# Forget gates of a streaming encoder step: float32 matmuls in four column blocks with a summing product, in place of 128-column float32r matmuls

## The reference, cut to what matters

```python
xn = rmsnorm(h, g_pre_mix)                    # h: (tokens, 1024)
y = jnp.einsum('bld,de->ble', xn, w_in)       # ... q_a | k_a | v_a | f_a (8 columns) | q_b ...
logf = jax.nn.log_sigmoid((f_a + b_forget).astype(jnp.float32))
# FoX: s = q k * scale + c_q - c_k, with c = cumsum(logf), causal; softmax; times v
```

## Time and profile before

| | |
|---|---|
| Median of 3 runs | 1680.81 us (1680.64 to 1680.95) |
| The profiled execution's own time | 1680.76 us |
| Its span (first to last instruction) | 1679.0 us |
| Granted TensorE clock, mean | 0.999 of full speed |
| TensorE busy | 1651.5 us (98%) |
| VectorE, ScalarE, GpSimd busy | 1083.5 us (65%), 775.8 us (46%), 310.2 us (18%) |
| DMA engines, mean over the span | 122 GB/s |

### The profile page before, as it was taken

How to read it: one execution, slowest core, us unless ns; L and a number is a source line. 1 busy time by engine, 2 the same in 40 slices (tenths; PEclk the granted TensorE clock), 3 DMA queues, 4 the chain that set the end, 5 groups by cost and what they waited for, 6 DMA issues and landing times.

```text
span 1679.0 us, 27411 instructions
## 1 busy us (share of the span) xinstructions
PE 1651.5 (98%) x9540; PEld 1489.3 (89%) x9540; DVE 1083.5 (65%) x2322; ACT 775.8 (46%) x1630; POOL 310.2 (18%) x438
## 2 busy tenths in 40 slices
PE   8999999999999999999999999999999999999998
PEld 8999999999999988989988899888888888888886
DVE  7556666553999744454445597888877667774744
ACT  6477777765777533352233333222222334443521
POOL 1311111115333211124532230000000000000242
PEclk9999999999999999999999999999999999999999
DMA  5221212231222554563443422444432763444641
GB/s 187 77 61 41 79 47 59 67 110 36 74 57 67 163 179 160 160 210 123 147 140 111 134 85 94 131 144 144 144 131 105 258 220 111 132 149 125 192 163 75
DMA packets 164314, 205.34 MB, mean 122 GB/s; under 512 B 16152, under 2 KB 113240, under 8 KB 164208
## 3 DMA queue, kind: packets, MB, share of 16 engines
q1 hardware_dynamic: 164208, 203.97, 38.0%
HBM read 144.85 MB, written 57.28 MB: 120 GB/s over the span
## 4 chain that ended last, share of the span: by engine, by line
PE 80%; DVE 9%; ACT 4%; issue 4%; POOL 2%; DMA 0%; DVEq 0%; ACTq 0%; SPq 0%; POOLq 0%
PE gb L503 8%; PE gb L3173 6%; PE gb L2290 5%; PE sc L3173 5%; PE gb L2825 4%; PE gb L2661 4%; PE sc L2825 4%; PE tp L3173 4%; PE tp L2825 4%; PE tp L798 3%; PE sc L2449 3%; PE tp L2449 3%; PE gb L930 3%; PE gb L931 2%; PE gb L932 2%
## 5 line engine op out<-in xcount | busy, mean ns | idle before, releaser
L930 PE MATMUL gb<-Xh,wh 128*128 128x384 f32 (+1 forms) x504 | 175.9, 349 | 0.0
L489 POOL TENSOR_TENSOR wl<-raw,wh 128x256 fp32r<-128x256 f32 x168 | 125.0, 775 | 264.2 <-ACT wh L474 175.4
L931 PE MATMUL gb<-Xh,wl 128*128 128x384 f32 (+1 forms) x504 | 170.7, 339 | 0.0
L932 PE MATMUL gb<-Xl,wh 128*128 128x384 f32 (+1 forms) x504 | 170.7, 339 | 0.0
L3297 POOL TENSOR_TENSOR wl<-raw,wh 128x1024 fp32r<-128x1024 f32 x2 | 5.3, 2626 | 559.0 <-ACT wh L3288 559.0
L503 PE MATMUL gb<-Xh,wh 128*128 128x384 f32 (+1 forms) x288 | 103.9, 361 | 0.0
L503 PE MATMUL gb<-Xh,wl 128*128 128x384 f32 (+1 forms) x288 | 97.4, 338 | 0.0
L503 PE MATMUL gb<-Xl,wh 128*128 128x384 f32 (+1 forms) x288 | 97.3, 338 | 0.0
L930 PEld LDWEIGHTS gb<-Xh,wh 128*128 128x128 f32 x504 | 95.0, 189 | 0.1
L931 PEld LDWEIGHTS gb<-Xh,wl 128*128 128x128 f32 x504 | 95.0, 188 | 0.0
L932 PEld LDWEIGHTS gb<-Xl,wh 128*128 128x128 f32 x504 | 94.8, 188 | 0.0
(11 more groups left out here) (548 smaller groups left out, 4777.4 us busy)
## 6 DMA issues: line engine op xcount, KB each, us to landing
zr<-u_scr SPq DMA_DIRECT2D x91, 256.0 KB, 3.0
raw<-in_w_in SPq DMA_DIRECT2D x70, 256.0 KB, 3.2
u_scr<-ustore SPq DMA_DIRECT2D x26, 576.0 KB, 3.6
u_scr<-ustore SPq DMA_DIRECT2D x13, 768.0 KB, 3.2
sig_scr<-sig SPq DMA_DIRECT2D x16, 576.0 KB, 3.1
raw<-in_w_up SPq DMA_DIRECT2D x36, 256.0 KB, 4.4
kc<-in_cache_fox_k SPq DMA_DIRECT2D x8, 1024.0 KB, 5.6
vc<-in_cache_fox_v SPq DMA_DIRECT2D x8, 1024.0 KB, 7.6
```

What stands on the lines that cost most here:

```text
L489: nc.gpsimd.tensor_tensor(wl[U.slot][:, q], raw[U.slot][:, q], wh[U.slot][:, q].bitcast(F32), ALU.subtract).then_inc(w_lo if x == 3 else w ...
L930: nc.tensor.matmul(gb[c][:, 0:x1 - x0], wh[U.slot][:, ws], Xh3[:, k, x0:x1], start=(k == 0), stop=False)
L931: nc.tensor.matmul(gb[c][:, 0:x1 - x0], wl[U.slot][:, ws], Xh3[:, k, x0:x1], start=False, stop=False)
L932: last = nc.tensor.matmul(gb[c][:, 0:x1 - x0], wh[U.slot][:, ws], Xl3[:, k, x0:x1], start=False, stop=(k == KT - 1))
```

## The change

The forget gates are multiplied in plain float32. `fw3` becomes 8 blocks of 32 columns (8 of weights, 24 of zeros), kept in `sig`; only 32 columns are loaded (`f_parts`). The 16 matmuls of `gates(c)` write four row groups of the bank: block k goes to rows 32(k mod 4) to 32(k mod 4)+31, so that each group sums two of the eight blocks, and four matmuls in a row go to four different groups. ACT copies all 128 rows of the bank into `f_sums`, which is `nB` (`f_sum_act`), and a 17th float32 matmul with a matrix of four small identities (`f_pick`, 8 columns) adds the four groups: `f_pick_pe(c)`, put behind `first(c)`. It writes rows 0 to 7 of the same bank, and DVE adds the bias from there. The turns move: 7, 8 and 9 are all in `first(1)`.

```diff
--- before.py
+++ after.py
@@ -377,7 +377,8 @@
 
 
 
-        fw = PTl[:, 8 * P:16 * P]
+        f_sums, f_pick, f_tmp = nB, sig[:, 0:8], sig[:, 16:64]
+        fw = sig[:, 64:320]
         fw3 = fw.rearrange("p (k n) -> p k n", k=KT)
         fbank = [po, gb[2], po]
 
@@ -400,8 +401,8 @@
         cst_in, cst_r, id_in, gpre_in = sem("cst_in"), sem("cst_r"), sem("id_in"), sem("gpre_in")
         x_in = [sem(f"x_in{t}") for t in range(10)]
         g_in, ssq_done, rstd_done, x_chain = sem("g_in"), sem("ssq_done"), sem("rstd_done"), sem("x_chain")
-        bf_in, lf_low, f_zero = sem("bf_in"), sem("lf_low"), sem("f_zero")
-        sq_done, xs_done, x_hi, x_lo = sem("sq_done"), sem("xs_done"), sem("x_hi"), sem("x_lo")
+        bf_in, f_summed, f_zero = sem("bf_in"), sem("f_summed"), sem("f_zero")
+        sq_done, xs_done, x_hi, f_picked = sem("sq_done"), sem("xs_done"), sem("x_hi"), sem("f_picked")
         lf_chain, lf_act, lf_done, cum_out = sem("lf_chain"), sem("lf_act"), sem("lf_done"), sem("cum_out")
         ckb_in = [sem(f"ckb_in{h}") for h in range(2)]
         zero_s, one_set, tail_zero = sem("zero_s"), sem("one_set"), sem("tail_zero")
@@ -448,6 +449,11 @@
             cs_ = bass.ds(reg * step + c0, P) if step else slice(c0, c0 + P)
             return [(lambda d: d[:, 0:4, :], v[:, 0:4, cs_]), (lambda d: d[:, 4:8, :], v[:, 4:8, cs_])]
 
+        def f_parts():
+
+            v = I["w_in"].rearrange("(k p) n -> p k n", p=P)[:, :, COL_F:COL_F + 32]
+            return [(lambda d: d[:, 0:4, 0:32], v[:, 0:4, :]), (lambda d: d[:, 4:8, 0:32], v[:, 4:8, :])]
+
         def cols_qb(reg):
 
             v = I["w_in"].rearrange("(k p) n -> p k n", p=P)
@@ -539,7 +545,7 @@
             rows_in(0, 1)
             sp.dma_start(gpre[:, :], I["g_pre_mix"].to_broadcast([P, D])).then_inc(gpre_in, 16)
             rows_in(2, 3)
-            load(sp, Unit(U_F), cols_of(I["w_in"], COL_F))
+            load(sp, Unit(U_F), f_parts())
             rows_in(4)
             load(sp, Unit(1), cols_of(I["w_in"], COL_QA))
             rows_in(5, 6, 7, 8, 9)
@@ -585,7 +591,7 @@
             square(3)
             root(1)
             high(0)
-            f_hi_act(act)
+            f_copy_act(act)
             high(1)
             square(4)
             high(2)
@@ -602,23 +608,35 @@
             square(9)
             high(6)
             root(4)
-            f_low_act(act, 0)
+            f_sum_act(act, 0)
             high(7)
             high(8)
-            f_low_act(act, 1)
+            f_sum_act(act, 1)
             high(9)
 
 
-        def f_hi_act(act):
+        def f_rows(k0):
+            return fw3[:, k0:k0 + 4, 0:8], raw[0][:, :].rearrange("p (k n) -> p k n", k=KT)[:, k0:k0 + 4, 0:8]
+
+        def f_copy_act(act):
             act.wait_ge(raw_full[0], 32)
             act.wait_ge(f_zero, 1)
-            nc.scalar.activation(fw3[:, :, 0:8], raw[0][:, :].rearrange("p (k n) -> p k n", k=KT)[:, :, 0:8],
-                                 ACT.Copy).then_inc(w_hi, 1)
-
-        def f_lo_pool(pool):
+            to, src = f_rows(0)
+            nc.scalar.activation(to, src, ACT.Copy).then_inc(w_hi, 1)
+
+        def f_copy_pool(pool):
+            pool.wait_ge(raw_full[0], 32)
+            pool.wait_ge(f_zero, 1)
             pool.wait_ge(w_hi, 1)
-            nc.gpsimd.tensor_tensor(fw3[:, :, 32:40], raw[0][:, :].rearrange("p (k n) -> p k n", k=KT)[:, :, 0:8],
-                                    fw3[:, :, 0:8].bitcast(F32), ALU.subtract).then_inc(w_lo, 1)
+            to, src = f_rows(4)
+            nc.gpsimd.tensor_copy(to, src).then_inc(w_lo, 1)
+
+        def f_pick_dve(v):
+            four_id = ident[:, :].rearrange("p (g r) -> p g r", g=4)
+            two = f_tmp[:, 0:16].rearrange("p (g r) -> p g r", g=2)
+            nc.vector.tensor_tensor(two, four_id[:, 0:2, 0:8], four_id[:, 2:4, 0:8], ALU.add).then_inc(f_zero, 1)
+            v.wait_ge(f_zero, 2)
+            nc.vector.tensor_tensor(f_pick, f_tmp[:, 0:8], f_tmp[:, 8:16], ALU.add).then_inc(f_zero, 1)
 
         def hi_second(act):
             act.wait_ge(raw_full[0], 64)
@@ -671,9 +689,10 @@
                                             ALU.subtract).then_inc(tp_free[h], 1)
 
             nc.vector.memset(small[:, :], 1.0).then_inc(x_chain, 1)
-            nc.vector.memset(fw.bitcast(F32), 0.0).then_inc(f_zero, 1)
+            nc.vector.memset(fw, 0.0).then_inc(f_zero, 1)
             v.wait_ge(id_in, 16)
             nc.vector.tensor_copy(ident_r[:, :], ident[:, :]).then_inc(cst_r, 1)
+            f_pick_dve(v)
             inverse(0)
             newton(0)
             v.wait_ge(gpre_in, 16)
@@ -727,19 +746,25 @@
                     last.then_inc(tp_full, 1)
 
 
-            def gates(c, between=()):
+            def gates(c):
                 a, b = CHUNK_ALL[c]
                 if c == 0:
                     pe.wait_ge(w_lo, 1)
                 if c == 2:
                     pe.wait_ge(bank_free[0], 1)
-                for k in range(KT):
+                for k0 in (0, 4):
                     for j, x_ in enumerate((Xh3, Xl3)):
-                        last = nc.tensor.matmul(fbank[c][:, 0:b - a], fw3[:, k, :], x_[:, k, a:b],
-                                                start=(k == 0 and j == 0), stop=(k == KT - 1 and j == 1))
-                    if k % 2 and k // 2 < len(between):
-                        between[k // 2]()
+                        for g in range(4):
+                            last = nc.tensor.matmul(fbank[c][32 * g:32 * g + 32, 0:b - a], fw3[:, k0 + g, :],
+                                                    x_[:, k0 + g, a:b].bitcast(F32),
+                                                    start=(k0 == 0 and j == 0), stop=(k0 == 4 and j == 1))
                 last.then_inc(gemm_done, 1)
+
+            def f_pick_pe(c):
+                a, b = CHUNK_ALL[c]
+                pe.wait_ge(f_zero, 3)
+                pe.wait_ge(f_summed, c + 1)
+                nc.tensor.matmul(fbank[c][0:8, 0:b - a], f_pick, f_sums[:, a:b], start=True, stop=True).then_inc(f_picked, 1)
 
             def first(c, between=()):
                 a, b = CHUNK_ALL[c]
@@ -768,12 +793,13 @@
             turn(2)
             turn(3)
             in_motion(20)
-            turns = (((), (4, 5, 6)), ((7,), (8, 9)), ((), ()))
+            turns = ((4, 5, 6), (7, 8, 9), ())
             for c in range(3):
                 for h in range(2):
                     pe.wait_ge(tp_free[h], 3 * c + 4)
-                gates(c, [lambda t=t: turn(t) for t in turns[c][0]])
-                first(c, [lambda t=t: turn(t) for t in turns[c][1]])
+                gates(c)
+                first(c, [lambda t=t: turn(t) for t in turns[c]])
+                f_pick_pe(c)
 
         class Count:
 
@@ -827,20 +853,19 @@
 
 
 
-        def f_low_act(act, c):
+        def f_sum_act(act, c):
 
             a, b = CHUNK_ALL[c]
             act.wait_ge(gemm_done, first_done(0, c))
-            nc.scalar.activation(le[:, a:b], fbank[c][32:40, 0:b - a], ACT.Copy).then_inc(lf_low, 1)
+            nc.scalar.activation(f_sums[:, a:b], fbank[c][:, 0:b - a], ACT.Copy).then_inc(f_summed, 1)
 
         def lf_dve_z(v, c):
 
             a, b = CHUNK_ALL[c]
             if c == 0:
                 v.wait_ge(bf_in, 16)
-            v.wait_ge(lf_low, c + 1)
-            nc.vector.scalar_tensor_tensor(lz[:, a:b], fbank[c][0:8, 0:b - a], bf, le[:, a:b],
-                                           ALU.add, ALU.add).then_inc(bank_free[c], 1)
+            v.wait_ge(f_picked, c + 1)
+            nc.vector.tensor_scalar(lz[:, a:b], fbank[c][0:8, 0:b - a], bf, None, ALU.add).then_inc(bank_free[c], 1)
 
         def lf_dve(v):
 
@@ -3508,7 +3533,7 @@
             hi_second(act)
             for c in range(2):
                 q_keep(act, 1, c, 0)
-            f_low_act(act, 2)
+            f_sum_act(act, 2)
             lf_act_(act)
             for y in range(2):
                 q_split_act(act, 0, y)
@@ -3713,7 +3738,7 @@
 
         @block.gpsimd
         def _(pool):
-            f_lo_pool(pool)
+            f_copy_pool(pool)
             for n in range(1, 5):
                 lo(pool, Unit(n))
             fox_keep_pool(pool, 0, 1, q_kept, qTs, nA[0], -1.0)
```

## The result

| | |
|---|---|
| Median of the changed kernel, 4 runs | 1689.88 us (1689.57 to 1690.84) |
| Median of the kernel before beside it, 4 runs | 1680.72 us (1679.77 to 1680.95) |
| Ratio, 95% interval | 1.0057 [1.0039, 1.0074] |
| The profiled execution's own time, its span | 1689.86 us, 1688.1 us |
| Mean granted TensorE clock | 0.998 |

The change costs 9.2 us between the medians; the ratio, formed from the runs' means, puts it at 0.57%. The forecast was 1687.6 with a range up to 1689.4: the sign was right, the median lies 2.3 us above the forecast and 0.5 above the range.

What follows compares the result with a forecast made beforehand. TensorE, busy 98%, bounds the kernel, and DVE's forget-gate chain before Unit 3 has no slack. The profiled 1680.76 us plus 6.85 for the later chain, other edits at nothing, gave 1687.6 us, range 1684.3 to 1689.4.

Steps and rivals of the forecast that it cites:

- Turn 9's wait: In first(1), TensorE waits 0.45 us for DVE to scale tile 9, until 40.45 us.
- The chain: DVE's forget-gate chain, without slack, starts behind pick 2 at 51.25 instead of 43.89 us, delaying key copy and Unit 3.
- the term of 6.85: Delay in us of DVE's key copy and Unit 3's weight load, added whole to the kernel's time.
- A visit to the four-block form: TensorE going in and out of four side-by-side matmuls: 0.35 us a visit, about 0.18 each side, four visits.
- TensorE's own lateness: At Unit 2's start, TensorE alone is 3.8 us late: 51.2 instead of 47.37 us.
- The edits at nothing: Smaller memset, f_pick additions, weight copies and 32-column load cost 0; the load's bounds were -1.2 and +0.3 us.
- case A: The forecast: the chain behind pick 2 decides, Unit 3 waits 3.2 us, time 1687.6 us; chance 0.69.
- rival B: The clock falls in the new standstills, 1.6 us a fall: 1689.2 us, or 1690.8 if twice; chance 0.10.
- all moved alike: Everything behind Unit 3 hangs on it, DVE or ACT and shifts equally, with no slack of absolute time left.
- C: Only TensorE's own 3.8 us count, the key copy being done in time after all: 1684.6 us; chance 0.09.
- D: Float32 fours cost one column time, 0.18 us a group: 1682.8 us, no measurable change; chance 0.06.
- E: The four matmuls run one after another, 10.7 us a chunk: 1711 us; chance 0.02.

Runs made afterwards that it cites:

- e3: Changed kernel with DVE's first two key copies issued inside the forget-gate chain, ahead of the running sum: 1684.88 us, ratio 1.0025.
- e2: Changed kernel with pick 2 moved from behind first(2) into it, after its second block: 1685.31 us, ratio 1.0028.
- e4: Kernel before, with only DVE's forget-gate chain held back until first(2) is done: 1686.88 us, ratio 1.0034.
- e12: Kernel before, with only 32 instead of 128 columns loaded for the forget gates: 1681.17 us, ratio 1.0000.
- e1: Changed kernel with 28 unread transposes filling TensorE's standstill before Unit 3: 1690.06 us, ratio 1.0052.
- e13: Changed kernel with both standstills filled, 14 transposes before pick 0 and 28 before Unit 3: 1688.46 us, ratio 1.0045.
- e14: Changed kernel with only pick 0's standstill filled, by 14 transposes: 1688.39 us, ratio 1.0046.
- e9: Changed kernel run again unaltered on another chip, five runs: 1688.31 us beside 1681.20, ratio 1.0041.
- e5: Kernel before, with 72 more idle transposes at the very start, so everything behind runs later: 1687.35 us, ratio 1.0034.
- e7: Kernel before, with DVE's first two key copies issued early inside the forget-gate chain: 1681.01 us, ratio 1.0001.
- e15: Changed kernel with early key copies and pick 0's standstill filled by 14 transposes: 1684.43 us, ratio 1.0021.
- e10: Changed kernel with 28 unread transposes before Unit 3, run again on another chip, five runs: 1687.37 us, ratio 1.0041.
- e8: Kernel before, with early key copies and the scaling of tile 7 moved from DVE to GpSimd: 1681.00 us, ratio 1.0000.

## Why the prediction was right in its sign and short in its size

**The head, step by step.** Nearly every row came where it was put. The fours: 0.67 and 0.65 us apart, forecast 0.67 and 0.64. Pick 0: 31.58 for 31.7. Its two records overlap with the fours of `gates(1)`, which start at 31.71, but `first(1)` still begins at 34.92 for 35.1. Turn 9's wait: 0.32 for 0.45. Unit 2: 51.01 for 51.2. The chain: 51.12 for 51.25. The key copy: 66.28 for 66.45. Unit 3: 66.96 for 67.1, standstill 2.85 for 3.2. So the term of 6.85 was 6.67. (The forecast counted the standstill from start to start; counted so it was 3.0, since 2.85 leaves out the last product's way through the array.) A visit to the four-block form was dearer in the forecast than in the trace: pick 2 starts 0.27 us behind the product before it instead of 0.18, and Unit 2 0.74 behind pick 2 instead of 0.64, 0.2 us in all for a term of 0.35. The bounds of the forecast do not add up by their own terms either: all of them together give 1685.0 to 1688.4, not 1685.6 to 1688.5. TensorE's own lateness, 3.8 in the text, is 3.6 at Unit 2 and 3.5 in e3, where nothing else is left; the chain behind pick 2 brings the rest, as e2, e3 and e4 each show by another way. The edits at nothing were at nothing (e12 for the load).

**The step that failed is the clock.** The forecast's case A set Unit 3's standstill at 3.2 us and let TensorE go on at full speed behind it; the fall stood apart as rival B with a chance of 0.10, on the reading that the trace was silent there. The two cases were one mechanism: A's own standstill is B's cause. And the trace was not quite silent: behind its last product TensorE stands idle from 1671.6 us, and there the granted clock falls:

```profile
1671.60:1675.20 3.60, 0.00 (x0) 1.00 0.19 76
1675.20:1679.00 3.80, 0.00 (x0) 0.51 0.36 138
```

That is a fall behind 3.7 us of idling in the profile of before; 3.2 us are close to it, and a chance of 0.10 was far too little. In the runs, the fall came behind Unit 3 in three of four profiled executions and behind pick 0 in two of six. B's price came out: 1.6 us forecast, 1.4 measured behind Unit 3 (8.1 against 6.7 in e1, 6.6 in e13 and e14), 1.5 to 1.6 behind pick 0 (e2, e9). That has luck in it, since the row it was taken from does not show a fallen clock: in the profile of before the transposes that start at 2.73 us run at half pace while the granted clock reads 1.00 (last section). A chance of some 0.7 for the first fall and 0.3 for the second, worked out from these counts, puts 1.5 us more on A. The Trainium skill's page TensorE: Matmul & The Clock Gate, Why this matters for your kernels, which warns of half rate behind idle gaps between bursts, agrees in kind with the rows of 66.9 to 69.9 us above; the gaps it names are longer than the 1.94 us behind which the clock fell in e2, and here the measurement decides.

**The other step that failed is "all moved alike".** 6.7 for the head and 1.4 for a fall make 1688.9 over 1680.76, which is still inside the range. The first set of runs lay at 1689.9 (the second at 1688.3), and what took it out is the last stage, a term put at nothing: there the profile loses 1.4 us, 1.1 of it in waits for data at 1392 and 1395 us. Such waits, 0.2 to 2.3 us long, come and go near 1383 to 1395 us in kernels made from either version, e5, e7 and e12 among them. "All moved alike" holds for the order of events, not for loads whose arrival varies by a microsecond while TensorE has no slack. Why they come late more often in some kernels isn't settled; this part of the cause stays open. Nor is the gain of 0.2 to 2.1 us settled that the shifted kernels show in the sliding-window attention. TensorE waits for `es` there in seven places of the profile after (4.1 us in all, 0.95 us at most) and as long before the change, but only 2.8 us in e1, which gains 2.1; the gain is there in e5 without any new instruction, but no run isolates it.

**The rivals.** B is told above. C (only TensorE's own, 1684.6) is refuted by the standstill; e3 (1684.9) and e15 (1684.4) made its case, and its number was good. D is refuted by the fours at 0.67 us, and so is E. The Trainium skill's 4x of TensorEngine Tiling (Array Packing), Theoretical Speedup, is there: four products side by side take 0.65 us over 384 columns where pick 2, one product alone, takes 0.74. But it stands against the slower float32 form, so that a four over 400 columns takes 0.67 us where one float32r matmul takes 0.18.

## What to carry to other kernels

Before a small product is put behind a long one on a full TensorE, look for what hangs on it elsewhere: here a matmul of 0.65 us moved a chain on two other engines by 7 us, and a weight load that came 0.19 us late had told that this chain had no slack. A forecast that makes a standstill of 2 to 3 us on a busy TensorE should take the fall of its clock into the sum, with a chance, at the 1.5 us that one cost here, and not as a separate case. Work of no use put into the standstill (transposes that nobody reads) kept the clock at 1.00 in the head of all six profiles that have it, though in time e1, e10 and e13 are not clearly faster than the changed kernel, while taking the dependence away, as with the early key copies, took 4.5 us of 8.

## What the runs showed of the hardware that I had not expected

- The granted clock fell to 0.50 (1.2 GHz) behind idle stretches of 1.94, 1.95, 2.28, 2.85, 2.87 and 3.19 us, and did not fall in others of 1.93 to 1.95 (four times) and 2.86 us (once). While there was work left, it fell nowhere in the seventeen profiles behind 1.51 us or less.
- Where it fell, it was sometimes already low when work resumed (0.3 us before in the first profile, 1.2 in e4) and sometimes fell 0.3, 0.5, 1.0 or 1.5 us into the work (e2, e1, e9 twice). Each fall lasted 3.4 us, the one in e4 6.8; the cost was 1.4 to 1.6 us in the head, in e4 2.6.
- Behind the program's last product, where TensorE has nothing more to do, the clock fell after 2.4 us in e14 and after 5.2 us in e15, and between these in the other fifteen profiles.
- At the start of the kernel before, 18 transposes took 3.7 us and the next 20 took 2.1, at a granted clock that reads 1.00 in both stretches. Why the first ones are slow, the rows do not show:

```profile
2.70:6.40 3.70, 3.67 (x18) 1.00 0.98 268
6.40:8.50 2.10, 2.10 (x20) 1.00 1.01 398
```

- Two different kinds of product run in each other's gaps: the 8-column pick's second record (31.92) comes behind the first records of the neighbouring 32-column four (31.71). Pick and gates together took 3.3 us (31.58 to 34.92) against 3.4 in the forecast, which put one after the other.
- On GpSimd, multiplying 128x1024 float32 by a number for each partition took 3.94 us, longer than multiplying it by another tensor, 2.38 us (e8; the profile's spans on GpSimd are rough):

```profile
24.45 3.94 POOL L3722 TENSOR_SCALAR xt<-xt,small 128x1024 f32<-128x1024 f32 x1 [4.54 <-DVE small L646]
28.46 2.38 POOL L3724 TENSOR_TENSOR xt<-xt,gpre 128x1024 f32<-128x1024 f32 x1
```
